# Sink-softmax attention in a hybrid encoder step: normalising probabilities by products with scaled identities

## The reference, cut to what matters

```python
def _sink_softmax(s, sink):
    sink_b = jnp.broadcast_to(sink.astype(jnp.float32), s.shape[:-1] + (1,))
    pr = jax.nn.softmax(jnp.concatenate([s, sink_b], axis=-1), axis=-1)
    return pr[..., :-1]
...
    o = jnp.einsum('bnkgqs,bnskd->bnqkgd', pr.astype(vb.dtype), vb)
```

## Time and profile before

| what | value |
|---|---|
| median of 3 runs | 1479.52 us (1477.32 to 1481.76) |
| the profiled execution, its own time | 1479.36 us |
| its span in the trace | 1477.6 us, so 1.8 us lie around the span |
| attention's loop, first transposes to the first product after the last `outputs` | 407.77 to 434.70 us of the span |
| mean granted clock of TensorE | 0.997 of full speed |

### The profile page before, as it was taken

The page is one execution under the profiler, slowest core; times in us unless marked ns, Lnnn a source line. Parts: engine busy times, 40 slices in busy tenths (PEclk is TensorE's granted clock), DMA queues, the critical chain, the costliest instruction groups (busy, mean ns, idle before and its releaser), DMA issues.

```text
span 1477.6 us, 23174 instructions
## 1 busy us (share of the span) xinstructions
PE 1456.2 (99%) x7986; PEld 1280.1 (87%) x7986; DVE 1197.9 (81%) x1436; ACT 1019.8 (69%) x1291; POOL 40.5 (3%) x67
## 2 busy tenths in 40 slices
PE   7999999999999999999999999999999999999998
PEld 6999999999988888888888888888888888888788
DVE  7744545458885899998999989999989999999887
ACT  5433333356786777877877877777787777787776
POOL 2000000000000000000000000000000000000001
PEclk9999999999999999999999999999999999999999
DMA  9444444435413999999999999999999999999951
GB/s 358 174 143 164 143 147 143 157 136 193 165 42 129 387 373 376 372 394 392 362 384 386 361 401 369 360 405 376 373 398 361 392 364 395 391 362 401 379 201 36
DMA packets 65828, 437.69 MB, mean 296 GB/s; under 512 B 8644, under 2 KB 10308, under 8 KB 14705
## 3 DMA queue, kind: packets, MB, share of 16 engines
q1 hardware_dynamic: 62592, 426.87, 75.0%
q0 software_dynamic: 2768, 9.89, 2.6%
q10 hardware_dynamic: 416, 0.26, 0.1%
HBM read 428.22 MB, written 8.77 MB: 296 GB/s over the span
## 4 chain that ended last, share of the span: by engine, by line
PE 94%; DVE 3%; DMA 1%; ACT 1%; issue 1%; SPq 0%; DVEq 0%; ACTq 0%; POOLq 0%
PE PS L751 91%; PE PS L1194 2%; DMA s_raw<-in_w_trunk 1%; PE PS L1150 0%; DVE s_Sl L1275 0%; ACT s_Sh L446 0%; DVE s_G L1445 0%; DMA s_G<-rows_dram,s_ix 0%; DVE s_Al L1280 0%; DVE s_st L1535 0%; PE PS L1100 0%; DVE s_G L1440 0%; PE PS L1227 0%; PE PS L1047 0%; PE PS L953 0%
## 5 line engine op out<-in xcount | busy, mean ns | idle before, releaser
L1275 DVE TENSOR_TENSOR s_Sl<-s_raw,s_Sh 128x1024 fp32r<-128x1024 f32 x796 | 934.8, 1221 | 128.5 <-ACT s_Sh L446 126.6
L446 ACT ACTIVATE s_Sh<-s_raw 128x1024 fp32r<-128x1024 f32 x798 | 799.8, 1052 | 212.5 <-PE PS L751 206.1
L751 PE MATMUL PS<-s_Sh,s_Ah 128*128 128x512 f32 x1344 | 529.5, 394 | 0.3 <-DVE s_Al L1280 0.3
L751 PE MATMUL PS<-s_Sh,s_Al 128*128 128x512 f32 x1344 | 523.9, 390 | 0.0
L751 PE MATMUL PS<-s_Sl,s_Ah 128*128 128x512 f32 x1344 | 523.2, 389 | 0.0
L751 PE MATMUL PS<-s_Ah,s_Sh 128*128 128x320 f32 x1008 | 314.8, 312 | 2.5 <-DVE s_Al L1280 1.7
L751 PE MATMUL PS<-s_Ah,s_Sl 128*128 128x320 f32 x1008 | 312.0, 310 | 0.0
L751 PE MATMUL PS<-s_Al,s_Sh 128*128 128x320 f32 x1008 | 312.0, 310 | 0.0
L751 PEld LDWEIGHTS PS<-s_Sh,s_Al 128*128 128x128 f32 x1344 | 252.3, 188 | 53.1
L751 PEld LDWEIGHTS PS<-s_Sh,s_Ah 128*128 128x128 f32 x1344 | 252.4, 188 | 51.2 <-issue 0.5
L751 PEld LDWEIGHTS PS<-s_Sl,s_Ah 128*128 128x128 f32 x1344 | 252.6, 188 | 50.6
(11 more groups left out here) (213 smaller groups left out, 591.8 us busy)
## 6 DMA issues: line engine op xcount, KB each, us to landing
s_raw<-in_w_moe SPq DMA_DIRECT2D x336, 1024.0 KB, 6.4
s_raw<-in_w_trunk SPq DMA_DIRECT2D x63, 1024.0 KB, 4.9
y_dram<-s_G POOLq DMA_DIRECT2D x3, 512.0 KB, 4.0
s_xT<-in_xT SPq DMA_DIRECT2D x2, 640.0 KB, 15.6
s_G<-in_x_rows SPq DMA_DIRECT2D x2, 512.0 KB, 5.5
rows_dram<-s_G SPq DMA_DIRECT2D x4, 256.0 KB, 2.0
s_G<-y_dram SPq DMA_DIRECT2D x2, 512.0 KB, 7.4
out_y<-s_G SPq DMA_DIRECT2D x2, 512.0 KB, 2.9
```

The costliest lines, as they stand in the source:

```text
L446: nc.scalar.activation(Sh[:, q % NSPL, o:o + UNIT // 2], raw[:, q % NRAW, o:o + UNIT // 2], ACT.Copy).then_inc(hi_ready, 1)
L751: return nc.tensor.matmul(out, w, m, start=start, stop=stop, **kw)
L1275: last = nc.vector.tensor_tensor(Sl[:, q % NSPL, o:o + UNIT // 2], raw[:, q % NRAW, o:o + UNIT // 2], Sh[:, q % NSPL, o:o + UNIT // 2].bit ...
```

## The change

`transposed` multiplies each 128x128 block by a scaled identity in place of transposing it: out = block^T times diag(1/sum), so the division by the sum happens in the product. DVE no longer scales the probabilities in place; it writes five scaled identities (`dg`, 128 x 5 x 128, two slots) with one tensor-tensor operation of `ident` by `acc`, both broadcast. `p_ready` goes up by two at its end. For j = 1, 3 and 5 the rounding of `high_o` is done by DVE, inside `low_o`, as a copy from PSUM that waits for `pv_done` and is linked to the subtraction behind it. The wait for `oh_ready` counts ACT's roundings alone.

```diff
+DVE_OUT = (1, 3, 5)
...
+        dg = view(G, pb0 + 4 * 384 + 512, 10 * P, 10)
...
             def high_o(j):
+                if j in DVE_OUT:
+                    return
                 act.wait_ge(pv_done, j + 1)
                 nc.scalar.activation(Ah3[:, j, :], PS[:, PVBANK[j % 2], 0:T], ACT.Copy).then_inc(oh_ready, 1)
...
                     for blk in range(4):
                         src = psm[:, j % 2, P * n:P * n + P] if blk == 3 else pp[:, 2 * (j % 2) + n, P * blk:P * blk + P]
-                        last = nc.tensor.transpose(PS[:, 5 + n, P * blk:P * blk + P], src, ident[:, :])
+                        by = dg[:, 5 * (j % 2) + (n, n, 2 + n, 4)[blk], :]
+                        last = mm(PS[:, 5 + n, P * blk:P * blk + P], src, by, True, True)
                     last.then_inc(pT_done, 1)
...
                 link(nc.vector.reciprocal(acc, acc))
-                nc.vector.tensor_scalar(psm[:, j % 2, 0:192], psm[:, j % 2, 0:192], acc[:, 4:5], None, ALU.mult)
-                for h in range(2):
-                    nc.vector.tensor_scalar(pp[:, b0 + h, 0:256], pp[:, b0 + h, 0:256], acc[:, h:h + 1], None, ALU.mult)
-                    nc.vector.tensor_scalar(pp[:, b0 + h, 256:384], pp[:, b0 + h, 256:384], acc[:, 2 + h:3 + h], None, ALU.mult).then_inc(p_ready, 1)
+                nc.vector.tensor_tensor(dg[:, 5 * (j % 2):5 * (j % 2) + 5, :], ident[:, None, :].broadcast_to([P, 5, P]),
+                                        acc[:, :, None].broadcast_to([P, 5, P]), ALU.mult).then_inc(p_ready, 2)
 
             def low_o(j):
-                v.wait_ge(oh_ready, j + 1)
+                if j in DVE_OUT:
+                    v.wait_ge(pv_done, j + 1)
+                    link(nc.vector.tensor_copy(Ah3[:, j, :], PS[:, PVBANK[j % 2], 0:T]))
+                else:
+                    v.wait_ge(oh_ready, j + 1 - sum(d < j for d in DVE_OUT))
                 low(Al3[:, j, :], PS[:, PVBANK[j % 2], 0:T], Ah3[:, j, :], ol_ready)
```

## The result

The changed kernel takes 1483.97 us (median; 1483.1 to 1485.46) against 1479.58 us (1477.32 to 1481.76) of the kernel before: 1.0032 times as long, 95% interval 1.0023 to 1.0040, so 3.4 to 5.9 us slower: a small difference, but clear of the noise. Its profiled execution took 1484.71 us with a span of 1483.0 us.

The account below looks back on a forecast made before the run. The prediction took TensorE, busy 99% of the span, to bound the kernel. Longer products (+7.6 us) less covered waits for DVE (-1.4 us) gave +6.2 us, from 1479.36 to 1485.6 us; range 1482.5 to 1488.5.

Parts of the forecast that it names:

- TensorE's products: Attention loop: eight plain fp32 products take two records each, 0.95 us more in each of eight rounds, 7.6 us.
- The price of four: Rival: in the loop a plain fp32 product costs four transposes, +20.2 - 1.4 us, 1498.2 us; chance 0.03.
- The waits that the products cover: Loop: TensorE's four waits for DVE's division, 1.40 us in all, are covered by the added products.
- The gap behind the block: TensorE's loads stand still 0.17 us behind each round's transposes; taken as staying, 1.4 us less if it goes.
- the second rival: Loop: the 0.17 us gaps go and second records run at 0.105 us; +3.9 us, 1483.3 us; chance 0.15.
- DVE's division: Loop: one 0.74 us operation replaces five scalings of 1.16 us, saving 0.42 us of DVE a round.
- the third rival: DVE remains late in the loop, the broadcast operation costing 1.49 us; +7.0 us or so, 1486.4 us; chance 0.10.
- Not slower: Rival: the loop's extra passes are hidden and only the waits go, -1.4 us, 1478.0 us; chance 0.10.
- Nothing outside the loop: What follows the loop was to shift as a whole, as long as before; no size given.

Follow-up runs that it names:

- e3: The kernel before with each of the 64 transposes issued twice; loop 29.72 us against 24.57, time ratio 1.0040.
- e5: The changed kernel with its 64 products taken as one-record fp32r products of other data; loop 24.98 us against 24.57 before, one execution.
- e4: The kernel before without the five scalings of a round, so the output is not normalised; loop 23.04 us against 24.57, one execution.
- e1: The kernel before with its transposes as plain fp32 products with the unscaled identity, DVE still dividing; loop 30.30 us against 24.57, ratio 1.0036.

## Why the prediction was right

It was right in direction, mechanism and range; the forecast of +6.2 us was 0.5 too high by the loop and 1.8 too high by the first medians, and it lies above their interval of 3.4 to 5.9.

- **TensorE's products.** The term was 0.95 us a round from two records at 0.112 us. Measured: 0.94 us from block to `outputs` (1.98 against 1.04), pace (1.86 - 0.19)/15 = 0.111. e3 and e5 show that the second record is the cost: two transposes are nearly as slow as one plain product, and a product of one record is as fast as a transpose. The row of the first stage predicted this price within 1%.
- **The price of four**, the rule of the Trainium skill (TensorE: Matmul & The Clock Gate, Terms), isn't borne out: 0.94 us a round in place of 2.5. Sixteen records for eight products, at nearly the transposes' pace, make the transpose about twice as fast here, not four times.
- **The waits that the products cover.** I put them at 1.40 us, read from the products' line. TensorE's weight loads run ahead of its products, so the wait is seen in full only there: the same stop is 0.49 us for the loads and 0.25 for the products. The loads stood still for 2.5 us in five waits; 0.17 of each is the gap of any such place, which leaves 1.65, and the sixth wait adds 0.13. This is the mis-sized term: 8 x 0.94 - 1.78 = +5.74 is what the loop shows. TensorE's own round was 3.32 us for the same reason, not 3.39, and the new one is 4.26, not 4.34. e4 won back 1.53 of the 1.78, with ACT as the next bound.
- **The gap behind the block** was taken to stay at 0.17 us, or to go (the second rival). It stayed. The idle time reads 0.12 us behind plain products, but only because their loads are 0.05 us longer (0.19 against 0.14). From the start of the block's last load to the first of `outputs` it is 0.31 us in e1 (421.80 to 422.11) as in e3 (410.56 to 410.87). So it does not belong to the transposes' mode; what it does belong to stays open.
- **DVE's division** was to save 0.42 us a round; e5 shows 3.83 us for a round with a rounding, so 3.31 without the copy and its link (421.85 - 421.33 = 0.52 in the changed kernel), 0.33 less than before: the identities start 0.07 us later behind the reciprocal than a scaling does. The round with a rounding I had at 3.7. The cover was 4.26 us, so neither mattered, and DVE never was late (the third rival): TensorE waited 0.3 us for it in two places, which is the gap of 0.17 and no more.
- **Not slower** (the first rival) needed products of one record. e5 gives it those, and the loop is still 0.41 us longer. I had this rival at -1.4 us; by e5 it would have failed on the moved roundings, where DVE's round is 0.2 us longer than before.
- **Nothing outside the loop** changed, as said, within the 1.8 us by which that part varies.

## What to carry to other kernels

Before moving work from a late engine to another, take the other's own work in a round and add the move's cost: here 3.32 + 0.94 against 3.64, so at best 1.8 us of waits were bought with 7.5 us of TensorE. A transpose against an identity is cheaper than the same product in plain fp32 (1.04 against 1.98 us for eight, with the gap), so folding a scale into it isn't free; count records in the trace, two for a plain fp32 product, one for a transpose. Where an in-order engine waits for its own small results, interleaving two independent chains of them can gain more than removing an operation: here removing one gained 0.43 us, and interleaving on top of it 0.72 more.

## What the runs showed of the hardware that was not expected

- From a full-width load (128x128) to the first half-width one 0.31 us pass, behind transposes (e3) and plain fp32 products (e1) alike, and 0.26 behind fp32r products (e5, 416.60 to 416.86), where the steps inside a block are 0.11.
- At the start of a block the second transpose's load follows the first in 0.06 us (e3), later ones in 0.109.
- TensorE's queue isn't kept in strict order, other than said ahead: in the kernel before a load of the next `scores` starts at 423.31 us, ahead of the last two loads of `outputs` at 423.35. Nothing of the sum hangs on it.
- Products of fp32r with 128 columns keep the pace of one record of plain fp32, 0.111 us.
- A DVE scaling of 256 fp32 columns takes 0.64 us beside a GpSimd multiplication in SBUF and 0.34 us without it.
- A small DVE operation costs 0.08 us behind an independent one and 0.20 us behind the one that it reads.
